# A two-layer decoder step with a mixture of experts: low parts interleaved, filler matmuls added, the first gather widened and the last norm shared out

## The reference

```python
for l in range(DEPTH):                      # DEPTH = 2
    m_p, ... = token_mix(y_p, ...)          # pooling branch + S5 state-space branch, sigmoid gates, @ w_out
    y_p = layer_norm(ALPHA * y_p + m_p, ln1_g[l], ln1_b[l])
    if l % 2 == 0: f_p = swiglu(y_p, w_ffn_gate[j], w_ffn_up[j], w_ffn_down[j])
    else:          f_p = moe_swiglu(y_p, w_router[j], ..., top 2 of 8 experts, each 1024 -> 3584 -> 1024)
    y_p = layer_norm(ALPHA * y_p + f_p, ln2_g[l], ln2_b[l])
```

## Time and profile before

| | |
|---|---|
| median of 3 runs | 1723.08 us (1720.0 to 1723.42) |
| the profiled execution | 1723.49 us |
| its span in the trace | 1721.8 us |
| mean granted TensorE clock | 0.973 of full |
| PE busy, PEld busy | 1652.0 us (96%), 1399.0 us (81%) |
| DVE, ACT, POOL busy | 1330.0, 978.2, 52.8 us |
| bytes read from memory | 437.06 MB, 255 GB/s over the span |

### The profile page before, as it was taken

How to read it: one execution, slowest core, us unless ns; L and a number is a source line. 1 busy time by engine, 2 the same in 40 slices (tenths; PEclk the granted TensorE clock), 3 DMA queues, 4 the chain that set the end, 5 groups by cost and what they waited for, 6 DMA issues and landing times.

```text
span 1721.8 us, 25165 instructions
## 1 busy us (share of the span) xinstructions
PE 1652.0 (96%) x9411; PEld 1399.0 (81%) x9411; DVE 1330.0 (77%) x1440; ACT 978.2 (57%) x886; POOL 52.8 (3%) x89
## 2 busy tenths in 40 slices
PE   7999988998999998999999999999999999999994
PEld 3887888998889787888888888888888888888883
DVE  5834557667575465998988988988998988989986
ACT  1222344442444235777777777777777777777771
POOL 2001000000001102000000000000000000000001
PEclk9998999999999898999999999999999999999997
DMA  6444544545353335899999999998998998998981
GB/s 163 124 120 88 161 147 145 172 160 172 95 167 102 82 126 196 308 361 357 329 375 339 344 369 328 358 376 325 342 384 322 350 379 314 371 370 313 370 335 25
DMA packets 209693, 441.80 MB, mean 257 GB/s; under 512 B 22896, under 2 KB 26912, under 8 KB 209614
## 3 DMA queue, kind: packets, MB, share of 16 engines
q1 hardware_dynamic: 205230, 434.40, 72.0%
q0 software_dynamic: 2432, 5.34, 1.7%
q10 hardware_dynamic: 1968, 1.19, 0.3%
HBM read 437.06 MB, written 1.93 MB: 255 GB/s over the span
## 4 chain that ended last, share of the span: by engine, by line
PE 82%; DVE 10%; issue 3%; DMA 2%; ACT 1%; SPq 0%; DVEq 0%; ACTq 0%; POOL 0%
PE bank L1579 79%; PE bank L1582 3%; DVE ssm L952 2%; DVE w_lo L952 2%; DVE piece_lo L952 1%; DVE r_all L952 1%; ACT y_hi L889 1%; DMA piece<-in_w_out_dram 1%; DVE scr L952 1%; DMA r_all<-in_b_glu_dram 1%; ACT piece_hi L709 0%; DMA piece<-in_w_ffn_gate_dram 0%; DVE ssm L1383 0%; DVE y_lo L1473 0%; DVE r_all L1310 0%
## 5 line engine op out<-in xcount | busy, mean ns | idle before, releaser
L952 DVE TENSOR_TENSOR w_lo<-weights,w_hi 128x2048 fp32r<-128x2048 f32 x336 | 765.1, 2289 | 99.4 <-ACT w_hi L898 95.3
L898 ACT ACTIVATE w_hi<-weights 128x2048 fp32r<-128x2048 f32 x336 | 644.5, 1920 | 190.3 <-PE bank L1579 190.2
L1579 PE MATMUL bank<-w_hi,xg_hi 128*128 128x512 f32 x896 | 357.5, 399 | 2.7 <-DVE xg_lo L952 1.1
L1579 PE MATMUL bank<-w_hi,xg_lo 128*128 128x512 f32 x896 | 351.0, 392 | 0.0
L1579 PE MATMUL bank<-w_lo,xg_hi 128*128 128x512 f32 x896 | 350.1, 391 | 0.0
L1579 PEld LDWEIGHTS bank<-w_hi,xg_hi 128*128 128x128 f32 x896 | 168.9, 188 | 42.1 <-DVE w_lo L952 4.7
L1579 PEld LDWEIGHTS bank<-w_hi,xg_lo 128*128 128x128 f32 x896 | 168.8, 188 | 36.7
L1579 PEld LDWEIGHTS bank<-w_lo,xg_hi 128*128 128x128 f32 x896 | 169.1, 189 | 33.1
L952 DVE TENSOR_TENSOR piece_lo<-piece,piece_hi 128x1024 fp32r<-128x1024 f32 x106 | 126.7, 1222 | 76.1 <-ACT piece_hi L709 73.1
L709 ACT ACTIVATE piece_hi<-piece 128x1024 fp32r<-128x1024 f32 x106 | 109.8, 1055 | 116.4 <-PE bank L1579 93.7
L1579 PE MATMUL bank<-w_hi,hidT_hi 128*128 128x512 f32 x448 | 175.0, 391 | 0.0
(11 more groups left out here) (297 smaller groups left out, 2047.3 us busy)
## 6 DMA issues: line engine op xcount, KB each, us to landing
weights<-in_w_moe_gate_dram SPq DMA_DIRECT2D x112, 1024.0 KB, 7.3
weights<-in_w_moe_up_dram SPq DMA_DIRECT2D x112, 1024.0 KB, 7.2
weights<-in_w_moe_down_dram SPq DMA_DIRECT2D x112, 1024.0 KB, 6.6
piece<-in_w_in_dram SPq DMA_DIRECT2D x48, 512.0 KB, 3.8
piece<-in_w_ffn_gate_dram SPq DMA_DIRECT2D x22, 512.0 KB, 4.7
piece<-in_w_ffn_up_dram SPq DMA_DIRECT2D x22, 512.0 KB, 4.2
piece<-in_w_ffn_down_dram SPq DMA_DIRECT2D x22, 512.0 KB, 3.6
piece<-in_w_out_dram SPq DMA_DIRECT2D x16, 512.0 KB, 4.7
```

The lines of the kernel that those rows point to most:

```text
L898: act.activation(w_hi[s % PAIRS][:, :], ring_slot[:, :], ACT.Copy).then_inc(w_hi_ready, 1)
L952: return dve.tensor_tensor(out, a, b, op)
L1579: signals(pe.matmul(out, lhsT, rhs, start=start, stop=stop, skip_group_check=True), signal)
```

## The change

1. `s5_tables` with `before`: a `next_lo` follows the second and the third doubling of `powr` (before: one after the last), and three more stand inside the loop on `turn`. `residual`: one `next_lo` follows each of the four additions.
2. PE: a new `fill(ps, n)` of n filler matmuls; 6 in each trunk norm between the mean and the variance matmuls, and 6 in the mixer between the `y` tiles and the transposes.
3. The first gather: 12 matmuls of 512 columns into banks 0 and 1, one copy by ACT and one by DVE into `xrow`, 4 fillers, 8 transposes.
4. The last norm: two fused instructions for each large tile on DVE, `(row - mean) * gain` and `* scale + bias`. The tile of 8 tokens goes to POOL in three instructions. Stores of the large tiles are issued by SP (6) and ACT (2), the small one by POOL.

```diff
@@ s5_tables, DVE
                     n *= 2
-                if before:
-                    next_lo(before[0])
+                    if before and n > 4:
+                        next_lo(before[0])
...
                     complex_mul(pair(turn, n, n + 1), pair(turn, n // 2, n // 2 + 1), pair(turn, n // 2, n // 2 + 1),
                                 work_pair(1))
+                    if before and n > 2:
+                        next_lo(before[1])
@@ residual, DVE
                         ins = tt(rT[:, k:k + 2, :], x_hi[:, k:k + 2, :], x_lo[:, k:k + 2, :], ALU.add)
+                        next_lo((*key, 0))
@@ ahead of the passes, ACT and DVE
+            act.wait_ge(first_picked, 1)
+            act.activation(xrow[:, 0:512], bank[0][:, :], ACT.Copy).then_inc(first_row_by_act, 1)
             act.wait_ge(npass_ready, 1)
...
+            dve.wait_ge(first_picked, 2)
+            dve.tensor_copy(xrow[:, 512:D], bank[1][:, :]).then_inc(first_row_by_dve, 1)
             dve.wait_ge(npass_ready, 1)
@@ final_norm, DVE
-                for h, (_, m) in enumerate(TILES):
-                    row = acc[0:m, h, :]
-                    step(dve.tensor_scalar(row, row, mv[0:m, h, 0:1], Y[0:m, h:h + 1], ALU.subtract, ALU.mult))
-                    step(tt(row, row, lnb[0:m, 0, :], ALU.mult))
-                    tt(row, row, lnb[0:m, 1, :], ALU.add).then_inc(y_out, 1)
+                for h in range(2):
+                    row = acc[:, h, :]
+                    step(dve.scalar_tensor_tensor(out=row, in0=row, scalar=mv[:, h, 0:1], in1=lnb[:, 0, :],
+                                                  op0=ALU.subtract, op1=ALU.mult))
+                    dve.scalar_tensor_tensor(out=row, in0=row, scalar=Y[:, h:h + 1], in1=lnb[:, 1, :],
+                                             op0=ALU.mult, op1=ALU.add).then_inc(y_out, 1)
@@ the end, POOL
+            row = acc[0:NDEC, 2, :]
+            pool.wait_ge(lnb_in, 32)
+            pool.wait_ge(fscale_ready, 1)
+            pool.tensor_scalar(row, row, mv[0:NDEC, 2, 0:1], small3[12][0:NDEC, 2:3], ALU.subtract, ALU.mult)\
+                .then_inc(y_out_step, 1)
+            pool.wait_ge(y_out_step, 1)
+            pool.tensor_tensor(row, row, lnb[0:NDEC, 0, :], ALU.mult).then_inc(y_out_step, 1)
...
@@ mixer, layer_norm and the first gather, PE
+                fill(claim(("yt", l, 0)), 6)
                 wait_emptied(pe, ("y", l, 2))
...
                 ps = claim(("var", l, which))
+                fill(ps, 6)
                 for k in range(KD):
                     pe.wait_ge(squared, 4 * n + k // 2 + 1)
...
-                gather_tile(bank[pass_bank[("gather", n)]], n)
+                for h in range(3):
+                    for x in (xtok_hi, xtok_lo):
+                        mm(bank[n][:, :], pick[:, h, :], x[:, h, 512 * n:512 * n + 512], h == 0 and x is xtok_hi,
+                           h == 2 and x is xtok_lo, first_picked if h == 2 and x is xtok_lo else None)
+            fill(bank[pass_bank[("ye", 1)]], 4)
+            for n, copied in enumerate((first_row_by_act, first_row_by_dve)):
+                pe.wait_ge(copied, 1)
+                for kk in range(4):
+                    at = 512 * n + P * kk
+                    turn_over(bank[pass_bank[("gather", n)]][:, P * kk:P * kk + P], xrow[:, at:at + P], P,
+                              filled if kk == 3 else None)
```

More of the change, by code:

```diff
@@ L472, in trunk_kernel @@
         xg_hi_ready, hidT_hi_ready = map(sem, ("xg_hi_ready", "hidT_hi_ready"))
+        first_picked, first_row_by_act, first_row_by_dve = map(
+            sem, ("first_rows_picked", "first_row_by_act", "first_row_by_dve"))
         router_zero, gslot_zero = map(sem, ("router_tiles_zero", "gslot_zero"))
@@ L475, in trunk_kernel @@
             sem, ("xtok_hi_ready", "xtok_lo_ready", "xtok_lo_of_pool", "y_hi_ready", "spread_ready"))
-        fvar_ready, fstd_ready, y_out = sem("final_var"), sem("final_std"), sem("final_y")
+        fvar_ready, fstd_ready, fscale_ready, y_out, y_out_step, y_stored = map(
+            sem, ("final_var", "final_std", "final_scale", "final_y", "final_y_step", "y_stored"))
         def tile_in(eng, key):
@@ L517, in load_columns, with store_tokens @@
                 eng.dma_start(cols[at:at + n, :], src).then_inc(signal, 16)
+        def store_tokens(eng, h, which):
+            eng.wait_ge(y_out, h + 1)
+            for jl in which:
+                eng.dma_start(y_prompt[0].rearrange("(c j) n -> j c n", j=CHUNK)[4 * h + jl],
+                              acc[32 * jl:32 * jl + 32, h, :]).then_inc(y_stored, 16)
         def load_tokens(eng, h):
@@ L588, in _ @@
                         expert_weights(e, e + c * NE)
+            store_tokens(sp, 0, range(4))
+            store_tokens(sp, 1, range(2))
         @block.gpsimd
@@ L680, in _ @@
                 pool.dma_start(lnb[:, i, :], w[name][DEPTH - 1].partition_broadcast(P)).then_inc(lnb_in, 16)
-            for h, (_, m) in enumerate(TILES):
-                pool.wait_ge(y_out, h + 1)
-                if m == P:
-                    for jl in range(4):
-                        pool.dma_start(y_prompt[0].rearrange("(c j) n -> j c n", j=CHUNK)[4 * h + jl],
-                                       acc[32 * jl:32 * jl + 32, h, :]).then_inc(stored, 16)
-                        n_stored += 1
-                else:
-                    pool.dma_start(y_sample.rearrange("b o n -> (b o) n"), acc[0:m, h, :]).then_inc(stored, 16)
-                    n_stored += 1
+            row = acc[0:NDEC, 2, :]
[5 more added lines that the diff above has]
+            pool.tensor_tensor(row, row, lnb[0:NDEC, 0, :], ALU.mult).then_inc(y_out_step, 1)
+            pool.wait_ge(y_out_step, 2)
+            pool.tensor_tensor(row, row, lnb[0:NDEC, 1, :], ALU.add).then_inc(y_out_step, 1)
+            pool.wait_ge(y_out_step, 3)
+            pool.dma_start(y_sample.rearrange("b o n -> (b o) n"), row).then_inc(stored, 16)
+            n_stored += 1
             pool.wait_ge(rows_out, 16 * 2 * DEPTH)
@@ L693, in _ @@
             pool.wait_ge(stored, 16 * n_stored)
+            pool.wait_ge(y_stored, 16 * 8)
         @block.scalar
@@ L937, in _ @@
             act.activation(small3[11], small3[10], ACT.Sqrt).then_inc(fstd_ready, 1)
+            store_tokens(act, 1, range(2, 4))
         @block.vector
@@ L1276, in residual @@
                             ins.then_inc(summed, 1)
-            def rsqrt(y, std, v, t):
-                step(tt(t, y, y, ALU.mult))
-                step(tt(t, t, v, ALU.mult))
-                step(dve.tensor_scalar(t, t, -0.5, 1.5, ALU.mult, ALU.add))
-                step(tt(y, y, t, ALU.mult))
             def layer_norm(l, which):
@@ L1539, in final_norm @@
                 step(dve.reciprocal(Y, STD))
-                rsqrt(Y, None, VAR, TMP)
-                dve.wait_ge(lnb_in, 32)
-                for h, (_, m) in enumerate(TILES):
-                    row = acc[0:m, h, :]
-                    step(dve.tensor_scalar(row, row, mv[0:m, h, 0:1], Y[0:m, h:h + 1], ALU.subtract, ALU.mult))
-                    step(tt(row, row, lnb[0:m, 0, :], ALU.mult))
-                    tt(row, row, lnb[0:m, 1, :], ALU.add).then_inc(y_out, 1)
+                step(tt(TMP, Y, Y, ALU.mult))
+                step(tt(TMP, TMP, VAR, ALU.mult))
+                step(dve.tensor_scalar(TMP, TMP, -0.5, 1.5, ALU.mult, ALU.add))
+                tt(Y, Y, TMP, ALU.mult).then_inc(fscale_ready, 1)
+                dve.wait_ge(fscale_ready, 1)
+                dve.wait_ge(lnb_in, 32)
+                for h in range(2):
[4 more added lines that the diff above has]
+                                             op0=ALU.mult, op1=ALU.add).then_inc(y_out, 1)
             angles()
@@ L1821, in keep_warm, with fill @@
                 wait_emptied(pe, key)
+                fill(bank[tiles.bank[key]], n)
+            def fill(ps, n):
                 for _ in range(n):
-                    mm(bank[tiles.bank[key]][:, 0:P], ident[:, :], ident[:, :], True, True)
+                    mm(ps[:, 0:P], ident[:, :], ident[:, :], True, True)
             def layer_norm(l, which):
@@ L1892, in _ @@
                        filled if h == 3 and hh == 2 else None)
-            def gather_tile(ps, n):
-                for kk in range(4):
-                    k = 4 * n + kk
-                    for h in range(3):
-                        for x in (xtok_hi, xtok_lo):
-                            mm(ps[:, P * kk:P * kk + P], x[:, h, P * k:P * k + P], pick[:, h, :],
-                               h == 0 and x is xtok_hi, h == 2 and x is xtok_lo,
-                               filled if kk == 3 and h == 2 and x is xtok_lo else None)
             keep_warm(("logits",), 8)
```

## The result

The changed kernel takes 1712.26 us (median of 4 executions, 1711.43 to 1713.3) beside 1723.25 for the kernel before (4 executions, 1720.0 to 1723.95); the ratio is 0.9937, with a 95% interval of 0.9922 to 0.9952. It is faster by 0.6%. The forecast was 1712.5, inside 1706 to 1717.5. The profiled execution took 1712.84, its span is 1711.1.

The account below looks back on a forecast made before the run. PE's work, its waits and its time at half clock were taken to bound the kernel; -2.5 - 4.2 - 2.6 - 1.2 - 1.3 + 1.2 = -10.6 from 1723.5 gave 1712.9, predicted as 1712.5 us, range 1706 to 1717.5.

Parts of the forecast that it names:

- Tables, -2.5: Low parts moved inside layer 1's tables: ninth piece 3.9 us earlier, less one likely low-clock spell; -2.5, bounds -3.9 and -1.4.
- Residual, -2.0 and -2.2: Low parts between the additions: PE's piece 1.9 us earlier, ahead of the feed-forward output (-2.0) and layer 1's `w_out` (-2.2).
- it isn't starved again: Residual: next low part comes every 1.8 us, PE needs 2.9 us for a piece, so no further wait.
- Mixers, -1.3 each: Fillers ahead of the mixer transposes keep the clock: -1.3 a layer, -2.6 for two, bounds -3.6 and 0.
- Norms, -1.2: Fillers ahead of the variance keep the clock, worth 1.7 in one norm; -1.2 in all, bounds -3.0 and +1.3.
- First gather, -1.3: Wide gather: passes start 0.6 us sooner, clock may return one spell earlier; -1.3, bounds -3.4 and +1.0.
- Last norm, +1.2: Fused instructions on DVE, small tile on POOL: +1.2 if the engines hold each other, -3.4 if free.
- Held in turn: Last norm: DVE's four fused instructions and POOL's three stand in a row, last store of the second tile at 1715.6.
- The engines do hold each other: Judges the rival that POOL and DVE don't hold each other at the end: last term -3.4, 1707.9 us; chance 25%.
- the fillers do hold the clock: Judges the rival that fillers don't: mixers give 0, norms +1.3, 1717.6 us; chance 15%.
- the tables gave back one spell and not two: Judges the rival that the table stretch gives all back by a longer wait and two low-clock spells: 1715.0 us; chance 12%.
- the 22 from which it would have decided: Slower rival: POOL's three instructions on 8 tokens end everything; from 22 us, instead of 6, they decide; chance 3%.

Follow-up runs that it names:

- no_mixer_fills: The changed kernel without the six fillers ahead of the transposes of each mixer, those of the norms kept; 1715.9 us, ratio 0.9964 to the kernel before.
- gather_only: The kernel before with the new first gather alone; ratio 0.9996 to the kernel before.
- layer_pool: The changed kernel with the nine loads of layer 1's tables issued by POOL and not SP; 1704.04 us, ratio 0.9883 to the kernel before.
- combined: The changed kernel with layer 1's loads on POOL, small tile on DVE, ACT's pass-count read before its row copy, residual low parts ahead of additions; 1694.44 us.
- combined_2: The kernel combined with the old first gather (48 matmuls of 128 columns, no row copies); 1699.59 us, ratio 0.9856 to the kernel before.
- tail_dve: The changed kernel with the tile of 8 tokens made by DVE in two fused instructions, none on POOL; 1707.02 us, ratio 0.9899 to the kernel before.

## Why the prediction was right, and where not

- **That PE's waits and clock set the time.** Right, and it was mostly the clock: the same matmuls took 11.3 us less, while the waits that no filler fills grew by 3.6, since PE now comes sooner to what others make. The two shares were not told apart in the sum.
- **The total.** By the table of places the terms were, in this pair of traces: tables -3.9, residual and `w_out` -3.0, mixers -1.6, norms -1.8, gather and the clock behind it -1.4, last norm +0.2, and +0.7 for the later start and what was lost ahead of the tables. Against -2.5, -4.2, -2.6, -1.2, -1.3 and +1.2 most terms are off by about a microsecond, and the errors cancel. The clock also moves a time by 5 us and more from one execution to the next. Hitting the median within 0.3 us was luck.
- **Tables, -2.5.** Right in mechanism: the ninth piece was expected at 320.4 and the tenth at 321.6, they came at 319.70 and 320.84 in a trace that starts 0.6 later, and the new wait is 2.12 instead of my 2.5. Mis-sized: it gave 3.9. I charged one spell of low clock to the new wait, and that spell is there (0.50 from 321.5 to 324.9, and so in ten traces of eleven). What I left out is that the old wait of 3.06 has two, with the clock at 0.51 from 296.5 to 303.4, and that one of them goes with it.
- **Residual, -2.0 and -2.2.** The first was right: 4.01 to 2.04. In the second the step "it isn't starved again" failed: after the first six records on a piece PE already wanted the next one and waited 0.76 more. The gap went from 3.38 to 1.64 + 0.76, worth 1.0.
- **Mixers, -1.3 each.** The size at the spot was 1.7 in both layers (118.01 instead of 119.71 behind the mark at layer 0's `w_glu`), and layer 1's lasted. The step that failed is that it would last: in layer 0 all but 0.2 of it was lost behind SP's ten microseconds of issuing small loads. I had not counted what is queued on SP ahead of `w_ffn_gate`. `no_mixer_fills` agrees: PE's first wait beside the tables comes 239.84 us behind the mark without these fillers, 240.30 with them.
- **Norms, -1.2.** They gave 1.8, nearly all in the second norm: from the mean's start to the variance's end 6.71 us instead of 8.46. Without fillers three traces of four have that loss, with them none of ten. In the third norm the clock holds either way (6.71 and 6.76). In the first the variance takes 3.75 instead of 5.74, but the fillers, at half clock (12 records took 2.75), delay it by about a microsecond, so 8.2 us instead of 9.0 are left, and those 0.8 us are gone again by PE's first wait beside the tables.
- **First gather, -1.3.** The start of the passes came 0.6 sooner and ACT was 1.4 late, both as worked out, and the clock came back sooner in the passes (-0.8): as a sum for this pair of traces it was right. The step that failed is a silent one: I compared with the old gather at the clock that it had in one trace. At full clock the old one is 1.4 us shorter, and `gather_only` shows no gain in the time.
- **Last norm, +1.2.** It was +0.2. "Held in turn" was wrong: one of DVE's four was held. The first of POOL's instructions, taken at 1.0, was 3.79 alone and 4.79 beside DVE. Two errors nearly cancelled, and the end was POOL's store, not that of DVE's second tile.
- **Rivals.** The engines do hold each other; the fillers do hold the clock in the mixers, and in the second norm; the tables gave back one spell and not two. POOL's chain ended 10.8 us behind the start of the last norm's fused part, half of the 22 from which it would have decided.

## What to carry to other kernels

Read what a timeline says of the clock as one draw of several: ask what an edit is worth at full clock and at half, and give it the gain only if both agree. When a wait is priced, count the spell of low clock behind the old wait as well as that behind the new one. Don't take the fall of PE's idle time for a gain where fillers went in. Follow a gain to the next thing that must arrive from outside: here nine small loads took SP, whose queue feeds the weights, ten microseconds, and moving them to idle POOL gave 4.4. Before work is given to an idle engine, time the instruction alone on it; 2.5 us of DVE's became 10 of POOL's.

## What the runs showed of the hardware

- POOL's `TENSOR_SCALAR` with two operands per partition on 8x1024 float32 takes 3.79 us alone, its `TENSOR_TENSOR` 2.33; DVE's fused instruction on 8x1024 takes 1.27, as on 128x1024.
- DVE and POOL hold each other only in part: 1.8 us on POOL's three and 0.8 on DVE's four. The Trainium skill (SBUF — State Buffer, "SBUF: two separate sides") describes an exclusive lock, held for the whole instruction, by which the other engine stands still. The runs agree that the engines hold each other, and don't show the strict turns that I drew from it: POOL's first runs from 1693.63 to 1698.42, and DVE's second ends and its third begins and ends inside that time.
- Two `cnat` loads of 128 KB took SP 4.57 us to issue in the changed kernel and the other two 3.01 (1.59 in the kernel before), POOL 1.51 and 1.50; why is open.
- A gap of 1.54 us on PE ahead of 36 small transposes cost the clock in eight cases of eight (2.75 to 3.6 us instead of 2.15); a gap of 1.57 ahead of the variance of the second and third norm did so in three cases of eight (5.5 us instead of 3.8).
- With layer 1's loads on POOL the kernel ends sooner behind its last instruction: in the changed kernel the span ends 6.8 us after POOL's last store starts, in `layer_pool` 4.9, and from the last statistics `combined` and `combined_2` take 18.2, `tail_dve` 20.1. Three traces of three show it; what it is stays open.
